# Scan stage of a hybrid decoder step: the weight split moves from POOL to ACT and DVE, and each weight tile is loaded a group ahead

## What is computed

```python
def ssd_scan(x, dt, a, b, c, h0):            # chunks of 128 tokens, 4 groups of 8 heads
    ...
    cs = jnp.cumsum(da, axis=2)
    xdt = xf * dtf[..., None]
    seg = cs[:, :, :, None] - cs[:, :, None, :]
    lmat = jnp.exp(jnp.where(mask, seg, -jnp.inf))
    scores = jnp.einsum('bclgn,bcsgn->bclsg', cf, bf)
    y_diag = jnp.einsum('bclsgh,bcsghp->bclghp', scores[..., None] * lmat, xdt)
    decay = jnp.exp(cs[:, :, -1:] - cs)
    st = jnp.einsum('bclgn,bclghp->bcghpn', bf, xdt * decay[..., None])
    ...
    y_off = jnp.einsum('bclgn,bcghpn->bclghp', cf, h_prev) * jnp.exp(cs)[..., None]
...
proj = u @ w_in
y = y + d_skip[:, None].astype(y.dtype) * xs
y_s = gated_rmsnorm(y.reshape(bt, L, SSM_INNER), sz, ssm_norm_w) @ w_s_out
y_m = (jax.nn.silu(mz) * o.reshape(bt, L, ATTN_W)) @ w_m_out
g = jax.nn.sigmoid(gr.astype(jnp.float32)).astype(x.dtype).reshape(bt, L, N_BRANCH, D_MODEL)
```

## Time and profile before

| | us |
|---|---|
| median of 3 runs | 2142.17 (2139.3 to 2142.96) |
| the profiled execution | 2143.95 |
| its span | 2141.8 |
| the scan stage, from the first product of its first tile (982.55) to the last product of its last group (1557.5) | 575 |
| pitch of a group: from the first x transpose (988.61) to the 32nd (1544.65), by 31 | 17.94 |

### The profile page before, as it was taken

One profiled execution on the slowest core, in us unless ns is written; L12 is line 12 of the kernel. 1 busy time (PEld: TensorE's weight loads), 2 busy tenths in 40 slices (PEclk: granted clock), 3 DMA queues, 4 the chain that ended last, 5 costly groups with the idle time before them and its releaser, 6 DMA issues.

```text
span 2141.8 us, 40632 instructions
## 1 busy us (share of the span) xinstructions
PE 2000.6 (93%) x13954; PEld 1911.0 (89%) x13954; DVE 1257.5 (59%) x2038; ACT 779.6 (36%) x1476; POOL 1022.6 (48%) x632
## 2 busy tenths in 40 slices
PE   3799999999999999896999999999979999999998
PEld 2799999999999999786888898889868999899986
DVE  6444544544543543594888888888862456765433
ACT  6344444444433333332555555555521111101021
POOL 4687887887877777272223122221222322333800
PEclk9999999999999999997999999999989999999999
DMA  4133333333322221345656564655585698643221
GB/s 130 52 114 98 110 105 99 108 104 102 98 66 62 69 62 46 107 125 192 207 151 208 161 199 153 208 169 175 183 260 160 188 299 240 224 167 136 87 99 70
DMA packets 343392, 299.46 MB, mean 140 GB/s; under 512 B 19415, under 2 KB 305735, under 8 KB 342273
## 3 DMA queue, kind: packets, MB, share of 16 engines
q1 hardware_dynamic: 268930, 201.14, 31.3%
q10 hardware_dynamic: 74410, 97.68, 13.4%
HBM read 222.50 MB, written 76.49 MB: 140 GB/s over the span
## 4 chain that ended last, share of the span: by engine, by line
PE 69%; DVE 14%; DMA 6%; issue 6%; ACT 2%; SPq 1%; ACTq 1%; POOL 0%; DVEq 0%; POOLq 0%
PE pm L1742 30%; PE acc L211 20%; PE acc L1742 8%; PE pm L1936 5%; DMA out_s_ssm<-arena 2%; DVE arena L1421 2%; DVE arena L1375 1%; PE pm L1866 1%; DVE arena L1467 1%; PE pm L1837 1%; DMA arena<-in_state_ssm 1%; PE pm L1883 1%; DVE arena L1420 1%; DVE arena L1464 1%; DVE ulo L1520 1%
## 5 line engine op out<-in xcount | busy, mean ns | idle before, releaser
L211 PE MATMUL acc<-uhi,whi 128*128 128x344 f32 x1560 | 523.9, 336 | 26.1 <-POOL wlo L204 21.7
L211 PE MATMUL acc<-ulo,whi 128*128 128x344 f32 x1560 | 505.0, 324 | 0.0
L211 PE MATMUL acc<-uhi,wlo 128*128 128x344 f32 x1560 | 504.9, 324 | 0.0
L202 POOL TENSOR_SCALAR whi<-raw 128x1024 fp32r<-128x1024 f32 x65 | 92.0, 1415 | 765.4 <-DMA raw<-in_w_in 436.7
L730 POOL TENSOR_TENSOR blo<-wraw,bhi 128x512 fp32r<-128x512 f32 x240 | 343.2, 1433 | 155.4 <-ACT bhi L835 155.4
L211 PEld LDWEIGHTS acc<-uhi,whi 128*128 128x128 f32 x1560 | 299.9, 192 | 36.1 <-issue 35.8
L211 PEld LDWEIGHTS acc<-uhi,wlo 128*128 128x128 f32 x1560 | 299.0, 192 | 7.0 <-issue 6.2
L211 PEld LDWEIGHTS acc<-ulo,whi 128*128 128x128 f32 x1560 | 299.2, 192 | 0.0
L1742 PE MATMUL pm<-slo,bhi 128*128 128x258 f32 x960 | 272.3, 284 | 0.0
L1742 PE MATMUL pm<-shi,bhi 128*128 128x258 f32 x960 | 271.9, 283 | 0.0
L1742 PE MATMUL pm<-shi,blo 128*128 128x258 f32 x960 | 271.8, 283 | 0.0
(11 more groups left out here) (310 smaller groups left out, 4179.7 us busy)
## 6 DMA issues: line engine op xcount, KB each, us to landing
wraw<-in_w_in SPq DMA_DIRECT2D x80, 512.0 KB, 4.7
raw<-in_w_in SPq DMA_DIRECT2D x33, 512.0 KB, 5.2
stage<-s_g SPq DMA_DIRECT2D x32, 516.0 KB, 4.0
arena<-s_cs SPq DMA_DIRECT2D x32, 512.0 KB, 5.1
s_g<-stage ACTq DMA_DIRECT2D x24, 516.0 KB, 2.8
s_xbc<-room ACTq DMA_DIRECT2D x24, 512.0 KB, 2.7
raw<-in_w_mem_kv SPq DMA_DIRECT2D x16, 512.0 KB, 3.8
arena<-s_xbc SPq DMA_DIRECT2D x32, 256.0 KB, 4.8
```

The lines of the kernel that those rows point to most:

```text
L202: pool.tensor_scalar(whi[r][:], raw[r][:], 1.0, 0.0, ALU.mult, ALU.add).then_inc(w_high[r], 1)
L211: mm = pe.matmul(out, w[r][:, k, :], a[:, k, c0:c0 + n], start=k == 0 and s == 0, stop=k == KT - 1 and s == 2)
```

## The change

- The split of the projection tiles in the scan stage leaves POOL. ACT rounds the half (`high_w`) of tile g+2 at the end of its group g, and DVE subtracts the rest (`low_main`) of tile g+1 in its group g, between the sample work and `outputs`. POOL has nothing to do in the stage.
- The first two weight tiles are loaded ahead of the loop. In the iteration of group g SP then loads the tile of group g+2, ahead of the inputs of group g. In the last two groups of the last chunk there is none to load.
- On DVE the skip product stands ahead of the sample work (`skip_part`), and in `outputs` the state is scaled first and added to third.

```diff
-            with sp.Fori(0, NCH) as c:
+            def load_group(c, last=False):
                 for g in range(GROUPS):
                     b, u = g % 2, c * 2 + g // 2
-                    load_w(sp, main_tile(c, g), cols_of(MAIN[g], c))
+                    if not (last and g >= 2):
+                        c2, g2 = c if g < 2 else c + 1, (g + 2) % GROUPS
+                        load_w(sp, main_tile(c2, g2), cols_of(MAIN[g2], c2))
                     sp.wait_ge(summed[b], u + OPEN)
...
+            for m in range(2):
+                load_w(sp, main_tile(0, m), cols_of(MAIN[m], 0))
+            with sp.Fori(0, NCH - 1) as c:
+                load_group(c)
+            load_group(NCH - 1, True)
...
-            with pool.Fori(0, NCH) as c:
-                for m in range(4):
-                    split_w(pool, main_tile(c, m))
...
                 if not first:
                     scale_y(c if g else c - 1, (g - 1) % GROUPS)
+                if nxt:
+                    high_w(main_tile(c if g < 2 else c + 1, (g + 2) % GROUPS))
+            for m in range(2):
+                high_w(main_tile(0, m))
...
+            def skip_part(c, g):
+
+                n = c * 4 + g
                 dve.wait_ge(gyn_ready, n + OPEN)
                 dve.tensor_tensor(heads(gy), heads(xt), bcast(dskip[:, g * HG:(g + 1) * HG], HD), ALU.mult).then_inc(y_step, 1)
+            def outputs(c, g):
+
+                n, b, u = c * 4 + g, g % 2, c * 2 + g // 2
                 dve.wait_ge(summed[b], u + 1 + OPEN)
+                dve.tensor_tensor(heads(hT[:, g, :]), heads(hT[:, g, :]), bcast(sm[:, 2, :], HD), ALU.mult).then_inc(h_scaled, 1)
                 dve.tensor_tensor(heads(yv), heads(pm[3][:]), bcast(sm[:, 1, :], HD), ALU.mult).then_inc(y_step, 1)
-                dve.tensor_tensor(heads(hT[:, g, :]), heads(hT[:, g, :]), bcast(sm[:, 2, :], HD), ALU.mult).then_inc(h_scaled, 1)
+                dve.wait_ge(h_scaled, n + 1)
+                dve.tensor_tensor(hT[:, g, :], hT[:, g, :], pm[0][:], ALU.add).then_inc(h_added, 1)
                 dve.wait_ge(y_step, n * 4 + 2)
                 dve.tensor_tensor(yv, yv, pm[4][:], ALU.add).then_inc(y_step, 1)
-                dve.wait_ge(h_scaled, n + 1)
-                dve.tensor_tensor(hT[:, g, :], hT[:, g, :], pm[0][:], ALU.add).then_inc(h_added, 1)
...
+            def low_main(c, m):
+
+                t = main_tile(c, m)
+                dve.wait_ge(w_high[t[1]], t[0] + 1)
+                dve.tensor_tensor(wlo[t[1]][:], raw[t[1]][:], whi[t[1]][:].bitcast(F32), ALU.subtract).then_inc(w_split[t[1]], 1)
             def dve_group(c, g, last=False):
 
                 operands(c, g)
+                skip_part(c, g)
                 if g % 2 == 0:
                     sample_step(c, g)
                 else:
                     sample_output(c, g - 1)
+                if not last:
+                    low_main(c if g < GROUPS - 1 else c + 1, (g + 1) % GROUPS)
                 outputs(c, g)
```

More of the change, by code:

```diff
@@ L1044, in norm_y, with act_group @@
                 act.activation(gyn, gy, ACT.Copy, scale=rs2).then_inc(gyn_ready, 1)
-            def act_group(c, g, first=False):
+            def act_group(c, g, first=False, nxt=True):
                 n = c * 4 + g
@@ L1065, in act_group @@
                     scale_y(c if g else c - 1, (g - 1) % GROUPS)
+                if nxt:
+                    high_w(main_tile(c if g < 2 else c + 1, (g + 2) % GROUPS))
+            for m in range(2):
+                high_w(main_tile(0, m))
             for g in range(GROUPS):
                 act_group(0, g, g == 0)
-            with act.Fori(1, NCH) as c:
+            with act.Fori(1, NCH - 1) as c:
                 for g in range(GROUPS):
                     act_group(c, g)
+            for g in range(GROUPS):
+                act_group(NCH - 1, g, nxt=g < 2)
             square_y(NCH * GROUPS - 1)
@@ L1459, in operands @@
                 dve.tensor_tensor(mm_, seg, scm.unsqueeze(1).to_broadcast([P, HG, CH]), ALU.mult).then_inc(m_ready, 1)
+            def skip_part(c, g):
+                n = c * 4 + g
+                dve.wait_ge(gyn_ready, n + OPEN)
+                dve.tensor_tensor(heads(gy), heads(xt), bcast(dskip[:, g * HG:(g + 1) * HG], HD), ALU.mult).then_inc(y_step, 1)
             def outputs(c, g):
                 n, b, u = c * 4 + g, g % 2, c * 2 + g // 2
-                dve.wait_ge(gyn_ready, n + OPEN)
-                dve.tensor_tensor(heads(gy), heads(xt), bcast(dskip[:, g * HG:(g + 1) * HG], HD), ALU.mult).then_inc(y_step, 1)
                 dve.wait_ge(summed[b], u + 1 + OPEN)
+                dve.tensor_tensor(heads(hT[:, g, :]), heads(hT[:, g, :]), bcast(sm[:, 2, :], HD), ALU.mult).then_inc(h_scaled, 1)
                 dve.tensor_tensor(heads(yv), heads(pm[3][:]), bcast(sm[:, 1, :], HD), ALU.mult).then_inc(y_step, 1)
-                dve.tensor_tensor(heads(hT[:, g, :]), heads(hT[:, g, :]), bcast(sm[:, 2, :], HD), ALU.mult).then_inc(h_scaled, 1)
+                dve.wait_ge(h_scaled, n + 1)
+                dve.tensor_tensor(hT[:, g, :], hT[:, g, :], pm[0][:], ALU.add).then_inc(h_added, 1)
                 dve.wait_ge(y_step, n * 4 + 2)
                 dve.tensor_tensor(yv, yv, pm[4][:], ALU.add).then_inc(y_step, 1)
-                dve.wait_ge(h_scaled, n + 1)
-                dve.tensor_tensor(hT[:, g, :], hT[:, g, :], pm[0][:], ALU.add).then_inc(h_added, 1)
                 dve.wait_ge(y_step, n * 4 + 3)
@@ L1500, in dve_group @@
                 inverse_root(c, g)
+            low_main(0, 0)
             decays(0, 0)
```

## The result

| | us |
|---|---|
| changed kernel, median of 4 runs | 2220.06 (2216.38 to 2226.86) |
| kernel before, same chip, median of 4 | 2141.52 (2139.3 to 2142.96) |
| ratio | 1.0371, 95% interval 1.0342 to 1.0400 |
| span of the profiled execution | 2215.8 (before 2141.8) |

The change makes the kernel 78.5 us slower. It was forecast to be slower by 38 us, with 2214 as the end of the range; the loss is twice the forecast one.

A forecast was written before the change was run, and what follows sets the result against it. The changed scan stage was taken to be bound by a loop through SP's loads: 10.8 + 8.5 + 9.8 + 9.6 = 38.7 us a pair, bringing group 31 38.0 us later, hence 2180 us; range 2146 to 2214.

The forecast's parts named there:

- The loop: Scan stage: inputs wait through SP's queue for DVE's subtraction, which needs the previous inputs; 38.7 us a pair against 35.9 before.
- the pitch of 16.5: Scan stage: PE's time per group when it waits for nothing, 16.5 us, or 33.0 a pair.
- The wait for the state: Scan stage, kernel before: PE's x transposes wait for DVE's state update, 28.7 us in 13 waits.
- a wait for s_cs: Scan stage: after the change, PE's x transposes idle about 2 to 3 us in every group until this input's DMA lands.
- L1421's successor: DVE's 128x1024 product in the scan stage: 3.37 us beside POOL's split, forecast at 1.22 after the change.
- The batches: SP's weight tile plus inputs, from weight-load issue to last landing: forecast 8.5 us behind even groups, 9.6 behind odd.
- my 8.0: Floor in us for SP's weight tile plus inputs, from a row with nothing before it, without ACT's traffic.
- it counts in full: Rival: ACT's traffic shares one pipe with SP's loads; 12 us behind odd groups, 9.0 behind even, 2222 us; chance 8%.
- The way to L1469: Loop's start, from x transposes to DVE's L1469 (L1459 before): 0.8 us to ACT's copy, then 3.2.
- ACT's rounding: One rounding per group, 1.05 us, forecast to hide at the group's end in ACT's wait for DVE's result.
- the port rule: Trainium skill: DVE and GpSimd lock a shared port pair, blocking two-input DVE operations; by it alone, 2098 us.
- my first rival: Rival: the loop doesn't bind, inputs come as early as before, PE runs at 16.5; 43.8 us gained, 2098; chance 3%.

## Why the prediction was right or wrong

**Right: the mechanism, its place and its sign.** The loop (inputs, decays, operands, sample work, subtraction, SP, inputs) sets the pitch. Opened at either of two places it is gone, and PE runs at the pitch of 16.5 that the prediction read from two rows. The wait for the state is replaced by a wait for s_cs, as said; L1421's successor takes 1.22 us; the span grew by 74.0 us and group 31 came 75.7 later, so the rest of the kernel is as it was to 2 us; groups 30 and 31 don't wait for inputs.

**Wrong: the size of the loop's terms, by 2.7 us a pair.** The sum step by step, as means over groups 2 to 28 of the changed kernel, worked out from the starts, issues and landings in its trace:

| term, us | predicted | measured | off |
|---|---|---|---|
| even group, landing of its inputs to weight load | 10.8 | 11.5 | 0.7 |
| batch behind it | 8.5 | 9.1 | 0.6 |
| odd group, landing of its inputs to weight load | 9.8 | 10.2 | 0.4 |
| batch behind it | 9.6 | 10.6 | 1.0 |
| pair | 38.7 | 41.4 | 2.7 |

14 pairs times 2.7 is 38 us. Group 1 starts 1.9 us sooner than forecast (1005.85 against 1007.8) and group 30 comes 1.6 later behind group 29 (18.1 us instead of 16.5), which nearly cancel. Group 31 is 37.7 us over its forecast of 1582.6, the median 40 over 2180. Two terms of the sum were too small.

*The batches (1.6 of 2.7).* I had the right cause, ACT's stores, and the right row for it, but scaled that row's 7.9 us by bytes from one transfer of 1376 KB to a batch of five. Moving the stores away took 2.3 us out of the batch behind odd groups and 1.5 out of that behind even ones. So the floor was lower than my 8.0 (7.6 behind even groups), and the stores cost more than the 1.6 and 0.5 that I gave them. The case "it counts in full" had 12 us behind odd groups, 1.4 too much where mine was 1.0 too little. That its pair of 41.6 and its time of 2222 come so near to the measured 41.4 and 2220 is in part luck: its batch was too long and its way to the weight load too short by nearly as much. The Trainium skill (DMA: Bandwidth & Descriptors, the sections on the specifications and on the anatomy of one DMA) gives some 358 GB/s for a core's share of HBM and about 2 us fixed, the latter for DMAs issued from GpSimd. The prediction's estimate from them, 6.8 us for the batch, lies below the shortest batch of any trace, 7.2; in the changed kernel the traffic of the other queue decided.

*The way to L1469 (1.1 of 2.7).* I followed ACT's path (copy of x, exponential) and left out that DVE itself has decays, inverse root and four operand instructions in its queue between the landing and L1469. In an odd group these take 4.46 us from the start of the transposes, with hardly an idle moment, against the 0.8 and 3.2 that I summed; in the first group of a chunk it is 5.0. ACT's path was shorter: its exponential ended 4.24 us behind the start of the transposes in groups 17 and 18 and 3.78 in group 19, and DVE's L1466, the last before L1469, ended at 4.54 or 4.55 in all three. Taking the root out brought 0.4 us in even groups.

**The price list of the other parts.** DVE's new order was priced at nothing beside the loop; by itself it is worth 6 us in the kernel before and nothing shown once PE is the bound. ACT's rounding was hidden, as said. The move of the split off POOL, which by the port rule and my first rival is the gain of the change, adds little once SP loads the tiles ahead, and with SP's old loop it loses 46 us (2187.8 against 2141.7). With POOL splitting, SP's order alone gives 2100.5 and both orders 2097.3, against 2095.1 and 2090.2 with the split on ACT and DVE. The Trainium skill (SBUF — State Buffer, the section on the two sides) has DVE and GpSimd shut each other out of a shared port for whole instructions. The rows agree: a product of 0.68 us took 2.83 beside POOL's subtraction, and ended within 0.6 us of it. But what that costs depends on when POOL is released, and the prediction took POOL's timing in the kernel before as given.

**The clock.** PE's lower granted clock is a companion, not a cause: 0.93 in the stage with the loop closed, 1.00 with it open, and in the changed kernel PE has slack in the loop. The first x transpose of groups 17 and 18 lasts 0.48 us, that of group 19 0.33, and L1469 comes 4.46 to 4.47 us behind its start in all three.

**What stays open.** How the stores' bytes come to cost 2.3 and 1.5 us is only known in part. The view by stretch has, inside the batch of group 17 of the changed kernel,

```profile
1350.00:1358.00 8.00, 5.86 (x37) 5.10 (x36) 3.86 (x6) 3.64 (x7) 0.00 (x0) 1.00 1.08 349
```

and inside the batch of the earlier trace rows that had nothing before it, in the kernel before,

```profile
976.00:981.00 5.00, 0.00 (x0) 0.00 (x0) 0.64 (x3) 0.00 (x0) 2.09 (x2) 0.50 1.08 323
```

The last two columns are the DMA engines' busy share and GB/s: the engines were fully busy with and without the stores, at nearly the same rate, which speaks for one rate that both queues share. How it is divided was not parted: 448 KB less of one store took 0.7 us off, 1028 KB moved away took 2.3. Why DVE idles 0.4 us before L1460 in the first group of a chunk, as in 1320.28 of the changed kernel, I don't know.

**The version to keep.** The inputs ahead of the weight tile in SP's loop, with or without the new order on DVE: 2095.1 and 2090.2 us, 2.2 to 2.3% faster than before. In this stage nothing but PE's own work is left.

## What to carry to other kernels

A load placed ahead on an in-order queue brings its wait along: before moving it, name what is queued behind it and follow who must run before the wait ends; if the way leads back to those transfers, that closed way is the new pitch. Put what has been free for long first, and what waits for the latest event last. When adding up such a loop, take on each engine the longer of the data's path and its own queue, and look for the other queue's stores in the same stretch before trusting a landing time measured alone.

## What the runs showed of the hardware that was not expected

A batch of 1664 KB in five DMAs on SP's queue landed in 7.6 us (mean of the even groups of the run with ACT's stores early) when ACT's queue stored 256 KB just before or beside it, and in 10.6 us when it stored 1284 KB in the same stretch. And PE's granted clock in the stage followed its gaps: 1.00 with PE busy for 527.75 of 528 us, 0.97 with 545.3 of 576, 0.93 with 571.78 of 652.
